# The front of an RWKV-7 time mixing: low-rank tiles over eight PSUM banks, r and v begun by halves, key work moved ahead

## The reference, cut to what matters

```
xx  = shift(u) - u                      # u: the normed input, shifted by a token
xs  = u + xx * mix[n]                   # six mixes: r, k, v, w, a, g
r, k, v = xs[0..2] @ w_in[0..2]         # three 1024x1024 products
w   = exp(-exp(-softplus(-(w0 + tanh(xw @ w1) @ w2)) - 0.5))
a   = sigmoid(a0 + (xa @ a1) @ a2);  g = sigmoid(xg @ g1) @ g2
kk  = k * k_k / norm of it per head
k   = k * (1 + (a - 1) * k_a)
state = state * w + (state @ -kk) (kk * a)^T + v k^T;   y = state @ r
```

## Time and profile before

| | |
|---|---|
| median of 3 runs | 2421.73 us (2420.33 to 2421.99) |
| the profiled execution | 2419.69 us |
| its span in the trace | 2417.9 us |
| TensorE busy | 2286.7 us, 95% |
| GpSimd busy | 1878.8 us, 78% |
| VectorE busy | 1321.3 us, 55% |
| ScalarE busy | 1020.9 us, 42% |

### The profile page before, as it was taken

One profiled execution on the slowest core, in us unless ns is written; L12 is line 12 of the kernel. 1 busy time (PEld: TensorE's weight loads), 2 busy tenths in 40 slices (PEclk: granted clock), 3 DMA queues, 4 the chain that ended last, 5 costly groups with the idle time before them and its releaser, 6 DMA issues.

```text
span 2417.9 us, 54595 instructions
## 1 busy us (share of the span) xinstructions
PE 2286.7 (95%) x20838; PEld 2219.8 (92%) x20838; DVE 1321.3 (55%) x1898; ACT 1020.9 (42%) x1499; POOL 1878.8 (78%) x1358
## 2 busy tenths in 40 slices
PE   8999999999999889999999788788999999999998
PEld 8999989999999889999999677668999999998998
DVE  6752147734762436753773966736771773335762
ACT  4344345344344435344343543325343434445442
POOL 6997828997997618997898587847997899755996
PEclk9999999999999989999999889999999999999999
DMA  5564524563553404564554332013564455433563
GB/s 191 174 201 130 183 63 150 175 199 123 178 195 124 144 13 147 174 205 129 170 189 156 97 113 88 3 38 105 182 191 165 147 177 193 145 122 97 183 199 113
DMA packets 90120, 348.74 MB, mean 144 GB/s; under 512 B 10016, under 2 KB 11808, under 8 KB 90016
## 3 DMA queue, kind: packets, MB, share of 16 engines
q1 hardware_dynamic: 90016, 347.31, 44.5%
HBM read 346.22 MB, written 1.05 MB: 144 GB/s over the span
## 4 chain that ended last, share of the span: by engine, by line
PE 75%; DVE 8%; POOL 8%; issue 5%; ACT 3%; DMA 0%; SPq 0%; POOLq 0%; DVEq 0%; ACTq 0%
PE bank L323 23%; PE bank L325 22%; PE bank L324 22%; POOL w_lo L1448 5%; POOL h L1482 2%; PE bank L737 1%; DVE cs L1938 1%; ACT w_hi L1061 1%; PE bank L590 1%; DVE m L1701 1%; DVE k_ L2029 1%; DVE a_ L2039 0%; PE bank L591 0%; DVE zneg L1789 0%; DVE zraw L1785 0%
## 5 line engine op out<-in xcount | busy, mean ns | idle before, releaser
L1448 POOL TENSOR_TENSOR w_lo<-raw,w_hi 128x512 fp32r<-128x512 f32 (+4 forms) x1152 | 1699.7, 1508 | 424.6 <-ACT w_hi L1061 406.4
L323 PE MATMUL bank<-x_hi,w_hi 128*128 128x272 f32 (+1 forms) x3280 | 956.7, 292 | 20.8 <-POOL w_lo L1448 12.1
L325 PE MATMUL bank<-x_hi,w_lo 128*128 128x272 f32 (+1 forms) x3280 | 951.1, 290 | 0.0
L324 PE MATMUL bank<-x_lo,w_hi 128*128 128x272 f32 (+1 forms) x3280 | 947.8, 289 | 0.0
L1061 ACT ACTIVATE w_hi<-raw 128x1024 fp32r<-128x1024 f32 (+2 forms) x608 | 667.1, 1116 | 261.4 <-PE bank L325 235.7
L323 PEld LDWEIGHTS bank<-x_hi,w_hi 128*128 128x128 f32 x3280 | 622.7, 190 | 29.0 <-issue 13.8
L324 PEld LDWEIGHTS bank<-x_lo,w_hi 128*128 128x128 f32 x3280 | 623.7, 190 | 0.2
L325 PEld LDWEIGHTS bank<-x_hi,w_lo 128*128 128x128 f32 x3280 | 622.8, 190 | 0.0
L323 PE MATMUL bank<-hid_hi,w_hi 128*128 128x272 f32 (+1 forms) x1408 | 404.6, 287 | 0.0
L325 PE MATMUL bank<-hid_hi,w_lo 128*128 128x272 f32 (+1 forms) x1408 | 404.3, 287 | 0.0
L324 PE MATMUL bank<-hid_lo,w_hi 128*128 128x272 f32 (+1 forms) x1408 | 403.6, 287 | 0.0
(11 more groups left out here) (320 smaller groups left out, 2465.2 us busy)
## 6 DMA issues: line engine op xcount, KB each, us to landing
raw<-in_ffn_in SPq DMA_DIRECT2D x352, 512.0 KB, 3.4
raw<-in_ffn_out SPq DMA_DIRECT2D x128, 704.0 KB, 4.1
raw<-in_sb_in SPq DMA_DIRECT2D x48, 512.0 KB, 3.5
raw<-in_rw_in SPq DMA_DIRECT2D x24, 512.0 KB, 3.5
raw<-in_sb_out SPq DMA_DIRECT2D x16, 512.0 KB, 3.4
raw<-in_mla_out SPq DMA_DIRECT2D x8, 512.0 KB, 3.5
raw<-in_rw_lora SPq DMA_DIRECT2D x8, 512.0 KB, 3.5
raw<-in_rw_out SPq DMA_DIRECT2D x8, 512.0 KB, 3.7
```

What stands on the lines that cost most here:

```text
L323: nc.tensor.matmul(o, wh, xh[:, k, cols()], start=start, stop=False)
L324: nc.tensor.matmul(o, wh, xl[:, k, cols()], start=False, stop=False)
L325: last = nc.tensor.matmul(o, wl, xh[:, k, cols()], start=False, stop=stop)
L1448: part = nc.gpsimd.tensor_tensor(w_lo[:, s, w], raw[:, s, w], w_hi[:, s, w], ALU.subtract)
```

## The change

- The outer low-rank tiles go over all eight banks, in the order 0, 1, 2, 3, 6, 7, 4, 5 in which `lora1`'s banks come free. The second `lora_input` stands between VectorE's steps, the fourth's activation on ScalarE behind the gates of w, and the second input has no activation pass of its own any more.
- The low parts of the inputs of k, r and v are made by VectorE (`low_of_mix`), tile by tile behind ScalarE's high parts (`high_of_mix`); GpSimd only splits weights in this stretch.
- The exclusive decay `ex3` is dropped: -kk is multiplied by `cs` shifted by one token (a wide product over tokens 1 to 271, and a small one for each chunk's first token). In its room lie `rx_hi` and `rx_lo`, which take r's first four tiles while k still runs.
- r and v begin by halves (`round_by_halves`): units 0 to 2 with tiles 0 to 3, then units 0 to 2 with tiles 4 to 7, then unit 3. v's tiles 0 to 3 go into `x_hi`, free by then, while r runs.
- The scaling of the sigmoids is folded into the exponentials. The key's factor, its square and its scaled copy are made tile by tile on ScalarE. The inverse decay, the roots and the decay stand between r's last evacuations. VectorE multiplies kk*a and the inverse decay before the bonus operand.

```diff
-                        return j % 4, s, lr, True, True
-                    return (4 * (s % 2) + j // 2) % 4, 2 + j % 2, lr, j % 2 == 0, j % 2 == 1
+                        return lora_order[j], s, lr, True, True
+                    return lora_order[4 * (s % 2) + j // 2], 2 + j % 2, lr, j % 2 == 0, j % 2 == 1
...
+                def receptances(s, j):
+                    return s, j, (rx_hi, rx_lo) if j < DT_ // 2 else x_parts, j == 0, j == 7
+                def round_by_halves(sec, block_of):
+                    base = n["x"]
+                    n["x"] += DT_
+                    order = [(s, k) for half in range(2) for s in range(3) for k in range(4 * half, 4 * half + 4)] + [(3, k) for k in range(DT_)]
+                    for s, k in order:
+                        if k == 0:
+                            pe.wait_ge(lo_ready, sec.start + s + 1)
+                            pe.wait_ge(bank_free[s], uses[s] + 1)
+                        if s == 0:
+                            pe.wait_ge(x_ready, base + k + 1)
...
                 def round_then_sums(sec):
-                    first_round(sec, False)
+                    round_by_halves(sec, receptances)
                     pe.wait_ge(rwc_loaded, 32)
                     uses_at["kk"] = list(uses)
-                    pe.wait_ge(kksq_ready, 1)
+                    pe.wait_ge(kksq_ready, DT_)
                     head_sums(range(8), 4, 4)
...
+                    for j in range(DT_):
+                        gate(0, j)
+                    inner(3)
                     ahead(0)
                     act.wait_ge(mixed_used, RING)
-                    parts_of_mix(k_)
+                    for j in range(DT_):
+                        gate(1, j)
+                        high_of_mix(0, k_, j, x_hi, j)
+                        if j == 3:
+                            ahead(1)
...
+                between = {("k", 0, 0): lambda: key_factors(0, 1, 2), ("k", 0, 1): lambda: key_factors(3, 4, 5), ("k", 0, 2): exponentials,
+                           ("k", 0, 3): lambda: receptance_parts(0), ("k", 1, 0): lambda: normed_keys(0, 1),
+                           ("k", 1, 1): lambda: normed_keys(2), ("k", 1, 2): lambda: normed_keys(3),
+                           ("r", 0, 0): lambda: normed_keys(4, 5), ("r", 0, 1): lambda: normed_keys(6, 7), ("r", 0, 2): lambda: value_parts(0),
+                           ("r", 1, 0): decay_inverse, ("r", 1, 1): kk_roots, ("r", 1, 2): decay}
...
-            def low_parts_of(src, ring=DT_):
-                for k in range(DT_):
-                    n["xhi"] += 1
-                    pool.wait_ge(xhi_ready, n["xhi"])
-                    nc.gpsimd.tensor_tensor(x_lo[:, k, :], src[:, k % ring, 0:L], x_hi[:, k, :], ALU.subtract).then_inc(x_ready, 1)
...
+                def low_of_mix(at, src, k, hi, lo):
+                    dve.wait_ge(part_hi_ready, DT_ * at + k + 1)
+                    nc.vector.tensor_tensor(lo[:, k, :], src[:, k, 0:L], hi[:, k, :], ALU.subtract).then_inc(x_ready, 1)
...
+                for k in range(DT_):
+                    low_of_mix(0, k_, k, x_hi, x_lo)
+                    if k % 2:
+                        gate_tile(k // 2)
...
+                for k in range(4):
+                    low_of_mix(1, r_, k, rx_hi, rx_lo)
+                written(sec_k.name_key, 8)
...
                 for k in range(DT_):
                     last = nc.vector.tensor_tensor_scan(cs[:, k, :], restart, w_[:, k, 0:L], 0.0, ALU.mult, ALU.add)
+                    if k == 3:
+                        for t in range(4, DT_):
+                            low_of_mix(1, r_, t, x_hi, x_lo)
...
+                for k in range(4):
+                    low_of_mix(2, v_, k, x_hi, x_lo)
+                dve.wait_ge(kkraw_ready, DT_)
+                dve.wait_ge(kksq_ready, DT_)
+                dve.wait_ge(key_factor_ready, DT_)
+                nc.vector.tensor_tensor(k_[:, :, 0:L], ex2[:, :, :], k_[:, :, 0:L], ALU.mult).then_inc(kprime_ready, 1)
                 for k in range(DT_):
                     b = 4 + k % 4
                     dve.wait_ge(head_sum, k + 1)
...
+                dve.wait_ge(pinv_ready, 1)
+                steps.link(nc.vector.tensor_tensor(a_[:, :, 0:L], a_[:, :, 0:L], ex2[:, :, :], ALU.mult))
                 dve.wait_ge(kkroot_ready, 1)
                 steps.link(nc.vector.tensor_tensor(m[:, :, :], m[:, :, :], ex[:, :, :], ALU.mult))
+                for k in range(4, DT_):
+                    low_of_mix(2, v_, k, x_hi, x_lo)
+                dve.wait_ge(pinc_ready, 1)
+                steps.link(nc.vector.scalar_tensor_tensor(w_[:, :, 1:L], m[:, :, 1:L], -1.0, cs[:, :, 0:L - 1], ALU.mult, ALU.mult))
+                steps.link(nc.vector.tensor_scalar_mul(w_[:, :, 0:L:TC], m[:, :, 0:L:TC], -1.0))
+                nc.vector.tensor_tensor(a_[:, :, 0:L], a_[:, :, 0:L], m[:, :, :], ALU.mult).then_inc(ops_ready, 1)
```

More of the change, by code:

```diff
@@ L178, in build @@
             ps = lambda name, shape, dt=F32: place.enter_context(nc.sbuf_tensor(name, shape, dt))
[L179 removed]
+            cs, ex, ex2 = (ps(n, [P, DT_, L]) for n in ("cs", "ex", "ex2"))
+            rx_hi, rx_lo = (ps(n, [P, DT_ // 2, L], F32R) for n in ("rx_hi", "rx_lo"))
         xplace.close()
@@ L1298, in time_mixing, with inner @@
                 nc.scalar.preload_act_table_set("sigmoid_and_others")
-                def body(i, ahead):
[L1301 to L1308, removed]
+                def inner(s):
+                    act.wait_ge(pre_ready, s + 1)
+                    if s != 1:
+                        nc.scalar.activation(lt[:, s, :], lt[:, s, :], ACT.Tanh if s == 0 else ACT.Sigmoid).then_inc(lt_ready, 1)
+                        act.wait_ge(lt_ready, max(s, 1))
+                    nc.scalar.activation(lr_hi[:, s, :], lt[:, s, :], ACT.Copy).then_inc(lhi_ready, 1)
@@ L1309, in time_mixing @@
+                def body(i, ahead):
+                    for s in range(RING):
+                        ahead(s)
+                        if s < 3:
+                            inner(s)
                 rounds(act, sec1, body, split_hi)
                 def body(i, ahead):
[L1312 to L1317, removed]
@@ L1343, in decay @@
                 def decay():
[L1344 to L1350, removed]
+                    nc.scalar.activation(cs[:, :, :], cs[:, :, :], ACT.Exp, scale=-DECAY).then_inc(pinc_ready, 1)
@@ new lines, in key_factors, with normed_keys, receptance_parts, value_parts @@
+                def key_factors(*tiles):
+                    for k in tiles:
+                        key_factor(k)
+                def normed_keys(*tiles):
+                    for k in tiles:
+                        normed_key(k)
+                def receptance_parts(half):
+                    for k in range(4 * half, 4 * half + 4):
+                        high_of_mix(1, r_, k, x_hi if half else rx_hi, k)
+                def value_parts(half):
+                    for k in range(4 * half, 4 * half + 4):
+                        high_of_mix(2, v_, k, x_hi, k)
@@ L1352, in body @@
+                for sec, dst, following_parts in ((sec_k, k_, receptance_parts), (sec_r, r_, value_parts), (sec_v, v_, None)):
                     def body(i, ahead):
                         for s in range(RING):
-                            if i == 1 and s == 3 and following_mix is not None:
+                            if i == 1 and s == 3 and following_parts is not None:
                                 act.wait_ge(unit_used, sec.start + sec.units)
-                                parts_of_mix(following_mix)
+                                following_parts(1)
@@ L1505, in time_mixing @@
                 rounds(pool, next(take), body, split_lo)
[L1507 to L1513, removed]
+                split_section()
+                for _ in range(3):
                     def body(i, ahead):
                         for s in range(RING):
-                            if i == 1 and s == 3 and following_mix is not None:
-                                low_parts_of(following_mix)
                             ahead(s)
@@ L1895, in lora_input, with gate_tile, written @@
                     nc.vector.tensor_tensor(lt[:, s, :], own[:, :], prev[:, 0:L], ALU.add).then_inc(pre_ready, 1)
+                def low_of_mix(at, src, k, hi, lo):
+                    dve.wait_ge(part_hi_ready, DT_ * at + k + 1)
+                    nc.vector.tensor_tensor(lo[:, k, :], src[:, k, 0:L], hi[:, k, :], ALU.subtract).then_inc(x_ready, 1)
+                def gate_tile(j):
+                    if j % 4 == 3:
+                        dve.wait_ge(unit_used, sec2.start + 3 + j // 4)
+                    else:
+                        dve.wait_ge(tile_done, 14 + 3 * (j // 4) + j % 4 + 1)
+                    b = lora_order[j]
+                    nc.vector.tensor_copy(g_[:, j, :], bank[b][:, 0:L]).then_inc(bank_free[b], 1)
+                def written(after, banks=4):
+                    for b in range(banks):
```

(12 more changed lines are left out.)

78 lines of the change are left out of this document (46 added, 32 removed).

## The result

The change makes the kernel slower: 2443.85 us (median of 4 runs, 2440.3 to 2444.7) against 2421.03 us beside it; the ratio is 1.0095, with a 95% interval of 1.0083 to 1.0107. The forecast was 2406, and 2398 to 2414 as its range. The profiled execution's span is 2441.5 us, 23.6 more than before.

The account below looks back on a forecast made before the run. TensorE, busy 95% of the span, was taken as the bound. Gains in the time mixing's front, 3 + 5 + 2.5 + 2.3 + 4 = 16.8, less 1, gave 2421.7 - 15.8 = 2406 us; range 2398 to 2414.

Parts of the forecast that it names:

- The token copies and sums behind v, and all that follows, stay: Work behind v's rounds in the time mixing and everything later: claimed unchanged, with no gain or loss.
- At nothing: Time mixing's front: key factors, squares and scaled keys on ScalarE, 24 operations of 0.33 to 0.42 us, priced at no gain.
- low clock spreading through the front: Rival, chance 0.05: many short waits keep TensorE at clock 0.50 for 72 us of the front; 21 us lost, 2427 us.
- low-rank product: Second stage of the low-rank product, over eight banks with second input earlier: ends near 1386 us, 3 us gained.
- k: k's matmuls, low parts made by VectorE, ready or within about 1 us: keeps 3.3 of 8.3 us lost, 5 gained.
- r's first round and the head sums: r by halves: input wait falls to 1.6 us, new wait of 5 to 7.5 at the head sums; 2.5 us gained.
- v's first round: v by halves: no wait for low parts at its head, unit 2's weights late; 2.4 us lost for 4.7, 2.3 gained.
- v's second round: Wide products done earlier, weight splits faster: three waits of 1.22 us go, 0.8 stays; 4 us gained.
- a low-clock stretch behind the new wait: After the new wait at the head sums, TensorE runs at the low clock for a stretch; 1 us taken off the gain.
- The first rival: Chance 0.16: weight splits delay VectorE's longer queue, TensorE waits 14 us at the head sums; 5 us gained in all, 2417 us.
- the four low-clock stretches: Stretches of TensorE at clock 0.50 in the front, 30.2 us together; each said to begin after TensorE had been waiting.
- The rule that was weighed: VectorE and GpSimd share an exclusively locked port pair, the loser fully blocked; named as speaking against the forecast.

Follow-up runs that it names:

- Without the moved tiles: The changed kernel with key_offset placed behind all others in the time mixing's own room, other tensors at their old addresses: 2405.29 us, ratio 0.9937 to the kernel before.
- the last edit of the experiments: VectorE's head-sum maxima put ahead of v's low parts and the key product, on the changed kernel with key_offset moved out from ahead of the ring: 2395.85 us.

## Why the prediction was wrong

**The step that failed** is the last of the change part by part: "The token copies and sums behind v, and all that follows, stay", and with it that everything ahead of 1366.5 us stays. The whole sum was made inside the front; what the change does to a program's other 2280 us was taken as nothing without being looked at. The tile `key_offset` is in no term of the sum: the key factors were priced as instructions, under "At nothing", and not as a tile with a place. That missing term is 37.7 us in the profiled execution and 38.6 between medians (2443.85 - 2405.29); what the runs showed in its place is VectorE's additions and products in the SwiGLUs, held up beside GpSimd's splits. None of the rivals named it; the one on the other side, low clock spreading through the front, did not come about either, as the granted clock of the stages above gives 0.89 or more, against 0.78 at the least in the earlier trace rows.

Without the moved tiles the kernel took 2405.29 us, close to the 2406 of the forecast, but in part by luck: in the table below k and r's first round gave 5.3 us less than forecast, the other rows 3.5 more.

**The front's terms**, by the stages of the earlier trace rows against those above:

| | forecast gain, us | measured, us |
|---|---|---|
| low-rank product | 3 | 22.6 - 19.3 = 3.3 |
| k | 5 | 32.5 - 31.2 = 1.3 |
| r's first round and the head sums | 2.5 | 27.4 - 26.5 = 0.9 |
| v's first round | 2.3 | 16.8 - 13.5 = 3.3 |
| v's second round | 4 | 16.9 - 12.2 = 4.7 |
| a low-clock stretch behind the new wait | -1 | r's second round, 12.1 - 12.8 = -0.7 |
| from v to the first gram | none | 8.6 - 7.4 = 1.2 |

*Low-rank product*: it ends near 1386 in the old count of time (1366.5 + 19.3 = 1385.8). The 7.4 us wait for w_ is gone; one of 2.9 for the third input stands in its place.

*k* was mis-sized. Its low parts were to stand ready "or within a wait of about 1 us". VectorE reached them at 1406.58, when k was due, and this row shows the rest:

```profile
1407.63 4.84 DVE L1955 TENSOR_TENSOR x_lo<-k_,x_hi 128x272 fp32r<-128x272 f32 x2
1412.40 0.43 DVE L1964 COPY g_<-bank 128x272 f32<-128x272 f32 x1
```

Two low parts of 0.44 us each took 4.84 beside the splits. TensorE waited 3.1 us for them and 0.9 for the copy of g before, and a lower clock followed (0.89 over k). The first rival was right on this mechanism here; at the head sums, where it put a wait of 14 us, there were 7.9.

*r and the head sums*: the wait was forecast at 5 to 7.5 us on VectorE's maxima and is 7.9. TensorE was to be there 15.6 us behind k's end and was there after 15.3 (1437.91 to 1453.2), the maxima were due after 20.5 to 23 and began after 22.8. The parts fit less well: those named with a price add up to 17 to 24.5, not 20.5 to 23, the four scans took 2.6 us for 4.4 to 6, and the 3.7 us that VectorE stood idle for ScalarE's high parts of v had no price:

```profile
1452.91 5.52 DVE L1955 TENSOR_TENSOR x_lo<-v_,x_hi 128x272 fp32r<-128x272 f32 x4 [3.69 <-ACT x_hi L1317]
1458.35 2.41 DVE L2024 TENSOR_TENSOR k_<-ex,k_ 128x2176 f32<-128x2176 f32 x1
1460.69 1.47 DVE L2028 TENSOR_SCALAR ex<-bank 128x272 f32<-128x272 f32 x4
```

The two rows ahead of the maxima are what the last edit of the experiments puts behind them. The gain is 0.9 and not 2.5 because the four sums behind the wait took 3.3 us at a granted clock of 0.50 (1.2 GHz), the first four 1.95 at 1.00; so most of the low clock for which the prediction took 1 us off fell into this row.

*v*: both rounds as forecast, a little better; the three waits of 1.22 us in the second are gone.

The scans, 2.83 us in the median in the earlier trace rows and taken at 1.16 bare by the first rival, are the one cost of VectorE's queue that nearly vanished, as few splits lie beside them now:

```profile
L2010 DVE TENSOR_TENSOR_SCAN cs<-consts,w_ x8: 692/693/2879, 1436.2 to 1446.4; 128x272 f32<-128x272 f32 x8
```

One reading of the prediction was loose, with no term resting on it: two of the four low-clock stretches did not follow a wait but began inside one (at 1372.1 and 1426.7 us, the waits of 7.4 and 6.7 us ending at 1375.6 and 1428.4).

**The rule that was weighed.** In the traces VectorE waits for whole splits: the addition's 0.43 us become 2.01 or 16.94, while the splits around it take 1.72 us each (12.04 for seven) in the one case and 1.67 (21.76 for 13) in the other. By the Trainium skill, "SBUF — State Buffer", section "Who interferes with whom", who issues first has the shared pair for its whole instruction and the other is fully blocked; the kernel before agrees, with one split at most in VectorE's way. The kernel after goes further than the rule as it stands there: a VectorE instruction already waiting was passed over for nine splits in a row. How the place of `w_lo` brings that about is open; the runs show that it does, and tried offsets of 32 and 64 bytes only.

## What to carry to other kernels

A new tile is an edit of every instruction whose operands lie behind it: put it behind the others, or keep them in place with a pad, and read the stages that the change does not touch before reading those that it does. Where VectorE adds two SBUF tiles beside a long run of GpSimd instructions, look at the longest of its durations and not at the median; if it is many times the rest, try moving GpSimd's output by 32 bytes or giving its run a gap; here both brought the longest back to 2.3 us. When a wait is forecast behind a list of work on one engine, ask which of that list the waiting engine needs: putting the maxima first was worth 9.4 us.

## What the runs showed of the hardware

- An addition of 0.43 us on VectorE lasted up to 17.9 us beside a run of GpSimd's splits without a gap, and whether it did hung on 32 bytes in the place of the tile that GpSimd writes: the kernel before took 2432 to 2450 us with it 32 bytes off, 2410 to 2422 with it in place or 64 off.
- With a gap after every second split it did not (longest 2.3 us; 2443.85 to 2419.77 us), though nothing had been moved.
- A scan of 128x272 takes 0.69 us where it meets no split; the least seen in the kernel before was 1.16.
